# An encoder layer on one core: four small first loads move from SyncE's queue to ScalarE's

## What is computed

```python
xn = rms_norm(x, norm1_g)
proj = xn @ w_in                      # 1024 x 1472, split for three mixers
x = x + concat[GLA(proj), Fourier(proj), MLA(proj)] @ w_out
x = x + hier_moe(rms_norm(x, norm2_g), ...)   # 32 experts, 2 per token
return rms_norm(x, final_norm_g)
```

## Time and profile before

| | |
|---|---|
| median of 3 runs | 536.99 us (536.18 to 537.57) |
| profiled execution, its own time | 537.57 us |
| its span in the trace | 535.7 us |
| TensorE busy | 496.4 us (93%) |
| VectorE / ScalarE / GpSimd busy | 208.3 / 137.3 / 81.8 us |
| bytes moved by DMA | 140.97 MB |

### The profile page before, as it was taken

The page is one execution under the profiler, slowest core; times in us unless marked ns, Lnnn a source line. Parts: engine busy times, 40 slices in busy tenths (PEclk is TensorE's granted clock), DMA queues, the critical chain, the costliest instruction groups (busy, mean ns, idle before and its releaser), DMA issues.

```text
span 535.7 us, 7660 instructions
## 1 busy us (share of the span) xinstructions
PE 496.4 (93%) x2932; PEld 271.9 (51%) x2932; DVE 208.3 (39%) x546; ACT 137.3 (26%) x327; POOL 81.8 (15%) x101
## 2 busy tenths in 40 slices
PE   4999999999999999999998899999999887888893
PEld 4446544569755554455545555555555443444321
DVE  2317220663576661126763322223322212322166
ACT  3504111352576661222221111111111110111022
POOL 1000000354000000001122322222233212211000
PEclk9999999999999999999999999999999998999998
DMA  8996000010595005921099999999999999999773
GB/s 275 361 278 247 1 1 0 16 36 2 193 414 217 2 2 214 399 93 41 7 370 338 418 414 416 414 417 418 416 414 417 416 416 415 418 415 410 309 320 158
DMA packets 40422, 140.97 MB, mean 263 GB/s; under 512 B 9880, under 2 KB 13016, under 8 KB 32192
## 3 DMA queue, kind: packets, MB, share of 16 engines
q1 hardware_dynamic: 35472, 132.58, 63.5%
q0 software_dynamic: 4816, 7.85, 4.0%
q10 hardware_dynamic: 96, 0.03, 0.0%
HBM read 131.49 MB, written 16.39 MB: 276 GB/s over the span
## 4 chain that ended last, share of the span: by engine, by line
PE 68%; DMA 18%; DVE 6%; SPq 5%; issue 2%; ACT 1%; DVEq 0%; ACTq 0%; POOLq 0%
PE bank L1056 14%; PE bank L741 12%; DMA EW<-in_moe_w_up 10%; PE bank L921 9%; PE bank L1069 7%; PE bank L904 4%; PE bank L967 3%; DMA XT<-in_final_norm_g 2%; PE bank L956 2%; PE bank L1029 2%; SPq L616 2%; PE bank L838 2%; DMA EW<-in_w_in 2%; DMA list_scratch<-lrow,dest 1%; PE bank L877 1%
## 5 line engine op out<-in xcount | busy, mean ns | idle before, releaser
L1056 PE MATMUL bank<-EW,WO 128*64 128x256 f32 x640 | 73.5, 382 | 10.4 <-DMA EW<-in_moe_w_up 9.2
L741 PE MATMUL bank<-EW,XT 128*128 128x512 f32 (+1 forms) x192 | 64.1, 495 | 0.0
L1056 PEld LDWEIGHTS bank<-EW,WO 128*64 128x64 f32 x640 | 45.1, 137 | 33.3 <-DMA EW<-in_moe_w_up 11.2
L1966 POOL DMA_INDIRECT y_scratch<-G,sidx x30 | 35.9, 1197 | 161.6 <-DVE G L1756 148.9
L921 PE MATMUL bank<-WO,XT 128*128 128x512 f32 x128 | 56.6, 595 | 0.0
L1383 ACT ACTIVATE G<-bank 128x128 f32<-128x128 f32 x32 | 8.9, 277 | 180.8 <-PE bank L1056 180.8
L1743 DVE TENSOR_TENSOR G<-G,bank 128x128 f32<-128x128 f32 x32 | 9.2, 287 | 101.6 <-ACT G L1383 101.6
L741 PEld LDWEIGHTS bank<-EW,XT 128*128 128x128 f32 x192 | 32.9, 190 | 31.0 <-issue 31.0
L1756 DVE COPY G<-bank 128x512 f32<-128x512 f32 x32 | 22.1, 692 | 59.8 <-PE bank L1069 59.8
L1069 PE MATMUL bank<-EW,G 128*64 128x512 f32 x160 | 38.6, 603 | 0.8 <-issue 0.8
L921 PEld LDWEIGHTS bank<-WO,XT 128*128 128x128 f32 x128 | 23.7, 190 | 27.3 <-issue 27.3
(11 more groups left out here) (288 smaller groups left out, 625.1 us busy)
## 6 DMA issues: line engine op xcount, KB each, us to landing
EW<-in_moe_w_gate SPq DMA_DIRECT2D x20, 1024.0 KB
EW<-in_moe_w_up SPq DMA_DIRECT2D x20, 1024.0 KB
EW<-in_moe_w_down SPq DMA_DIRECT2D x20, 1024.0 KB, 22.6
y_scratch<-MIX SPq DMA_DIRECT2D x8, 512.0 KB, 9.0
WO<-in_w_out SPq DMA_DIRECT2D x2, 2048.0 KB, 11.6
MIX<-in_moe_w_gate SPq DMA_DIRECT2D x4, 1024.0 KB
MIX<-in_moe_w_up SPq DMA_DIRECT2D x4, 1024.0 KB
WO<-in_moe_w_gate SPq DMA_DIRECT2D x4, 1024.0 KB
```

What stands on the lines that cost most here:

```text
L741: mm = pe.matmul(ps[:, 0:width], xnT[:, c, t * P:(t + 1) * P], w_in_sb[:, c, col:col + width], start=(c == 0), stop=(c == C - 1))
L1056: mm = pe.matmul(bank[BLOCK * m:BLOCK * (m + 1), 0:2 * P].rearrange("p (w n) -> p w n", w=2), xeT[:, buf, c, par * BLOCK:(par + 1) * BLOCK ...
L1966: pool.indirect_dma_start(y_rows, bass.IndirectOffsetOnAxis(ap=sidx[:, e:e + 1], axis=0), Y[:, e % 2], None, bounds_check=4 * S - 1, oob_i ...
```

## The change

The four small loads are taken from SyncE's list and put at the head of ScalarE's, ahead of its table load, in the order ident, gain1, small, posi. The semaphore and all waits stay as they were. SyncE's list now begins with the first tile of X.

```diff
@@ -549,12 +549,6 @@
         @block.sync
         def _(sp):
-            sp.dma_start(small[:, :], d["c_small"]).then_inc(first_landed, 16)
-            sp.dma_start(posi[:, :],
-                         d["positions"].rearrange("b (t p) -> p (b t)", p=P),
-                         allow_slow_non_contiguous=True).then_inc(first_landed, 16)
-            sp.dma_start(ident[:, :], d["c_ident"]).then_inc(first_landed, 16)
-            sp.dma_start(gain1[:, :], d["norm1_g"][0].rearrange("(p c) -> p c", c=C)).then_inc(first_landed, 16)
             for t in range(T):
                 sp.dma_start(X[:, t, :], x_v[:, t, :]).then_inc(x_landed[t], 16)
@@ -1207,6 +1201,12 @@
         @block.scalar
         def _(act):
             link = linker(act, act_chain)
+            act.dma_start(ident[:, :], d["c_ident"]).then_inc(first_landed, 16)
+            act.dma_start(gain1[:, :], d["norm1_g"][0].rearrange("(p c) -> p c", c=C)).then_inc(first_landed, 16)
+            act.dma_start(small[:, :], d["c_small"]).then_inc(first_landed, 16)
+            act.dma_start(posi[:, :],
+                          d["positions"].rearrange("b (t p) -> p (b t)", p=P),
+                          allow_slow_non_contiguous=True).then_inc(first_landed, 16)
             norms = [0]
```

## The result

| | median | runs |
|---|---|---|
| before, in the same comparison | 537.17 us | 536.18 to 538.03, 8 runs |
| changed | 539.77 us | 538.35 to 541.13, 8 runs |

The ratio is 1.0054, with a 95% interval of 1.0043 to 1.0066: the changed kernel is 2.6 us slower. Its profiled execution took 541.13 us with a span of 539.3 us, the slowest of its eight, as the profiled one of before was the slowest of three.

What follows compares the result with a forecast made beforehand. The start was taken as bound by SyncE's data stream, until w_in's first slice landed. Small loads at 10.0, transpositions from 10.1 plus 6.35 gave 16.4, less 13.51: +2.9; 536.99 + 2.9 = 539.9 us, range 536.9 to 541.8.

Steps and rivals of the forecast that it cites:

- SyncE 1.93 us earlier: On SyncE's queue, X's first issue moves from 2.68 to 0.75 us, so everything on that queue starts 1.93 us earlier.
- The small packets' own time: On the DMA engines, small packets beside X add up to 0.95 us; slice of w_in lands between 11.5 and 12.5.
- The landing of the small loads: On ScalarE's queue, small packets alternate one for one with SyncE's; last load lands at 9.5 to 10.9, taken as 10.0.
- rival B: DMA queues alternate in longer turns; small loads land by 8.1 us, first product +1.0 us, 538.0 us; chance 0.17.
- The transpositions: On TensorE, they start at 10.1 us and keep the old 6.35 us until the first product, at 16.4.
- ScalarE's issues, 0: On ScalarE, four issues ahead of the table load take about 1.89 us, ending it near 3.9 before tile 0; price 0.
- C: Small packets pass promptly on the DMA engines, landing by 5.5 us; 536.0, or 535.1 if time is hidden; chance 0.14.
- D: On the DMA engines, each small packet waits for two of SyncE's queue; +7 us, halfway +4.5 us; chance 0.09.
- The shift stays: After TensorE's first product with w_in, no later wait absorbs the start's shift; it counts in full, +2.9 us.

Runs made afterwards that it cites:

- e9: The changed kernel measured once more, unaltered; 539.43 us, ratio 1.0051 to before.
- e1: Changed kernel, but TensorE waits for ident alone and ScalarE for gain1 ahead of its copies; VectorE still waits for small and posi first; 537.46 us.
- e2: As e1, but VectorE makes the rope angles after its copies and the four diagonals; 535.65 us, ratio 0.9981 to before.
- e4: Half of the change: SyncE keeps ident and small ahead of X, ScalarE takes posi and gain1, one semaphore; 535.96 us, ratio 0.9979 to before.
- e6: Changed kernel, but posi is read as 128 rows of 16 bytes instead of 512 single integers; 537.64 us, ratio 1.0014 to before.
- e3: Changed kernel with the positions loaded a second time on ScalarE's queue, and all waits counting it; 540.67 us, ratio 1.0078 to before.
- e5: Changed kernel with ScalarE's four loads in the opposite order: posi, small, gain1, ident; 539.10 us, ratio 1.0044 to before.
- e7: Changed kernel, but small and posi on SyncE behind w_in's first slice, ident and gain1 with own semaphores, rope angles late; 534.36 us, ratio 0.9954 to before.
- e10: The kernel e7 measured once more, unaltered; 534.35 us, ratio 0.9950 to before.
- e12: The kernel e7 with 17 unused products on TensorE ahead of its wait for ident; 534.88 us, ratio 0.9958 to before.

## Why the prediction was right

**The result.** Predicted 539.9 us, measured 539.77. Much of that closeness is luck: in the trace the first product moved by 3.7 us (3.6 in e9), not 2.9, and in the medians the difference was 2.6 and 2.7. The start was 0.8 us worse than reckoned, and the medians moved by about 1 us less than the start did.

**SyncE 1.93 us earlier.** Right. X's first issue moved from 2.68 to 0.75 us, its first tile from 6.38 to 4.52, 1.86 earlier.

**The small packets' own time.** Mis-sized for the slice. It landed at 2.60 + 10.2 = 12.8 us, where the bound was 12.5: the packets cost 1.3 us of the stream, not 0 to 0.95. The last tile of X landed at 2.1 + 6.8 = 8.9, inside its bounds. As the first product no longer waited for the slice, it didn't enter the sum; for e1 and e2 it did.

**The landing of the small loads.** That TensorE would be held by the small loads' packets beside the stream is shown by e1, e4 and e6, and one for one by the counts of the changed kernel and of e3. It is not a rule of the two queues, as e5 shows. The size was 1.0 us short: 11.0 instead of 10.0, just beyond the range of 9.5 to 10.9. The term at fault is the pace beside the slice, taken as 0.060 us per packet. Of q10's 960 packets, 745 had passed by 9.0 us, when tile 3 had just landed: 47 per engine, near the 45 that the prediction had there at best. But the remaining 13 took until 10.5 us, 0.11 each, and landed at 11.0. From 9 to 10 us the counts were even and the engines were not full:

```profile
q1 hardware_dynamic: 157, 0.16, 59.9%
q10 hardware_dynamic: 158, 0.00, 8.4%
```

So an engine took 0.10 us for a pair of packets, one of each queue, and was idle for about a third of that; what it waited for, the profile doesn't show. In the third stretch of the result the pair took 0.075 us, in e3 0.049.

The Trainium skill ("DMA: Bandwidth & Descriptors", section "Queues, rings and completion order") has an engine drain a whole group of descriptors from one ring before it changes to the next. Posi would then have landed near 8.1 us, by rival B. The counts (200 to 218, 306 to 300, 319 to 317) and the 11.0 us don't bear that out in the changed kernel; the measurement decides. The 355 packets beside 22 in e5 are nearer to such turns than to an even alternation.

**The transpositions.** 6.21 us from their start to the first product instead of 6.35; they took 6.06 us, 25 of them 5.29. They were not faster although all of X lay there. That it came so near is partly luck: in e9, e5, e3 and e6, which begin in the same way, they took 5.95, 5.59, 5.27 and 5.16 us.

**ScalarE's issues, 0.** Right: its table load ended at 3.92, before X's first tile.

**The rivals.** B fell by the counts and by the landing, in the changed kernel. C fell in the changed kernel, and e4 shows when it holds: when the packets have passed before the stream fills. D fell, the ratio was 1.0 and not 1.5 or 2.

**The shift stays.** Right up to the experts: +3.71 us at 283.16. From the first product with w_in to the experts' first product it is 269.5 to 269.7 us in before, the changed kernel and every experiment but e1, whose first product stood alone. Behind that the shift is covered by scatter. From the experts' first product to the span's end it is 535.7 - 283.2 = 252.5 us before and 252.4 in the changed kernel, but 250.8 in e9 (537.4 - 286.6), 251.7 in e7 and 251.4 in e10; over all fourteen profiles it lies between 250.5 (e3) and 252.5. The profiled executions of before and of the changed kernel both lie at the long end. With 2 us of such scatter, a median can move by 2.6 where the trace of the start moves by 3.7, and e7's by 2.6 where its start moves by 1.8. Whether it is scatter alone or this stage also gets shorter in the edited kernels is open; there is only one profile of before. The falls of the granted clock don't settle it: before and e9 each had one of 3.4 us in this stage, apart from the end, and differ by 1.7 us.

## What to carry to other kernels

A load on a second queue is not free because it is small. Beside a full stream its packets took turns with the stream's in most stretches here, so count its packets per DMA engine and not its bytes: 512 single integers are 33 per engine and landed after 8.8 us, as 128 rows they are 9 and landed after 7.4. The time per packet is known only roughly, 0.05 to 0.11 us beside a stream of 1 KB packets. Moving such a load to the front doesn't help if the stream starts with it: in e5 it held the stream back instead. Start such loads while nothing streams, or behind what is urgent, and put on the second queue only what the first work needs. Before an early issue can pay, look at every wait on the moved loads' semaphore and at what is queued behind it: here TensorE waited for positions that it never reads, and VectorE's copies stood behind a chain that nobody needed until much later.

## What the runs showed of the hardware that I had not expected

In the changed kernel the even alternation counted completions too and held for packets from 4 bytes to 4 KB. In e5 it failed for a while: 355 packets of 4 bytes passed beside 22 of the stream's, and the stream fell to 0.05 MB in 1 us.

Alternation also slows the stream: beside 319 packets of almost no bytes the slice's stretch moved 0.34 MB in 1.5 us (0.23 MB per us), against 0.74 MB in 2 us alone, 0.37 per us. The engines were busy for 85% of that stretch, so the small packets' own 11.7% is not the whole price.

TensorE's transpositions ran at half pace, as 1.2 against 2.4 GHz, in stretches for which the granted clock reads 1.00. The clock column alone would have hidden it, because it has no record ahead of the first rise: 3.74 us for 32 of them after 6.8 us of unused products (e12), 5.2 to 6.5 us in the kernels where TensorE had been idle since the start.
